# Conditioning projections: one-column products moved from inside two feed-forward parts to the waits of two layer norms

## The reference, cut to what matters

```
x = layer_norm(ALPHA * x + 0.5 * swiglu(x, w_gu, w_down), g, b)    # four times
shared = nsa_shared_kv(x, nsa_w_kv, ...)                           # after layer 0
```

```
def ada_params(cond, w, b):
    m = jax.nn.silu(cond) @ w + b      # w: 1024 x 3072
    return jnp.split(m, 3, axis=-1)    # shift, scale, gate
hl = rmsnorm(xl, norm_g[l]) * (1.0 + scale) + shift
```

## Time and profile before

| | us |
|---|---|
| median of 3 runs | 2537.26 (2536.59 to 2537.66) |
| span of the profiled execution | 2533.9 |
| TensorE busy | 2492.8 (98%) |
| DVE busy | 1446.8 (57%) |
| POOL busy | 1081.5 (43%) |
| ACT busy | 955.0 (38%) |

### The profile page before, as it was taken

The page is one execution under the profiler, slowest core; times in us unless marked ns, Lnnn a source line. Parts: engine busy times, 40 slices in busy tenths (PEclk is TensorE's granted clock), DMA queues, the critical chain, the costliest instruction groups (busy, mean ns, idle before and its releaser), DMA issues.

```text
span 2533.9 us, 34230 instructions
## 1 busy us (share of the span) xinstructions
PE 2492.8 (98%) x12668; PEld 2007.6 (79%) x12668; DVE 1446.8 (57%) x2058; ACT 955.0 (38%) x1500; POOL 1081.5 (43%) x718
## 2 busy tenths in 40 slices
PE   8999999999999999999999999999999999999999
PEld 7888887657788888788888777788888888787887
DVE  6545556575755645555654648674343364896553
ACT  5222224464422223432222468653222244463322
POOL 3978874203749942323633402264020056032401
PEclk9999999999999999999999999999999999999999
DMA  8345445311444455344442221145333326533332
GB/s 212 95 128 150 126 123 138 97 34 51 125 125 132 149 145 133 107 133 125 141 150 85 82 80 34 51 147 168 107 107 94 94 75 191 190 124 112 92 92 67
DMA packets 439259, 292.07 MB, mean 115 GB/s; under 512 B 34371, under 2 KB 420218, under 8 KB 435802
## 3 DMA queue, kind: packets, MB, share of 16 engines
q1 hardware_dynamic: 422042, 212.38, 29.9%
q0 software_dynamic: 17088, 77.93, 9.8%
HBM read 272.50 MB, written 20.92 MB: 116 GB/s over the span
## 4 chain that ended last, share of the span: by engine, by line
PE 88%; POOL 5%; DVE 3%; ACT 2%; issue 1%; DMA 0%; SPq 0%; ACTq 0%; POOLq 0%; DVEq 0%
PE ps L770 40%; PE ps L775 20%; PE ps L853 5%; PE ps L880 4%; PE ps L1078 2%; PE ps L1066 2%; POOL SW L3145 1%; POOL NS L3143 1%; PE ps L1502 1%; POOL NS L3142 1%; DVE wl L2298 1%; PE ps L1093 1%; PE ps L1355 1%; PE ps L1259 1%; PE ps L1085 1%
## 5 line engine op out<-in xcount | busy, mean ns | idle before, releaser
L2298 DVE TENSOR_TENSOR wl<-raw,wh 128x1024 fp32r<-128x1024 f32 x376 | 617.9, 1644 | 839.8 <-ACT wh L1728 836.6
L1728 ACT ACTIVATE wh<-raw 128x1024 fp32r<-128x1024 f32 x385 | 408.2, 1060 | 1320.5 <-PE ps L775 1159.5
L770 PE MATMUL ps<-XH,wh 128*128 128x512 f32 x1832 | 719.2, 393 | 0.5 <-ACT wh L1728 0.5
L770 PE MATMUL ps<-XL,wh 128*128 128x512 f32 x1832 | 713.2, 389 | 0.0
L775 PE MATMUL ps<-XH,wl 128*128 128x512 f32 x1832 | 453.2, 389 | 0.0
L770 PEld LDWEIGHTS ps<-XH,wh 128*128 128x128 f32 x1832 | 344.0, 188 | 76.8 <-issue 4.9
L770 PEld LDWEIGHTS ps<-XL,wh 128*128 128x128 f32 x1832 | 344.0, 188 | 72.8 <-issue 2.2
L775 PEld LDWEIGHTS ps<-XH,wl 128*128 128x128 f32 x1832 | 343.9, 188 | 71.7 <-issue 0.4
L3264 POOL TENSOR_TENSOR NS<-AW,CS 128x2048 f32<-128x2048 f32 x32 | 116.8, 3649 | 215.8 <-PE ps L1173 207.1
L770 PE MATMUL ps<-HH,wh 128*128 128x512 f32 x528 | 207.2, 392 | 0.0
L770 PE MATMUL ps<-HL,wh 128*128 128x512 f32 x528 | 205.5, 389 | 0.0
(11 more groups left out here) (538 smaller groups left out, 3929.2 us busy)
## 6 DMA issues: line engine op xcount, KB each, us to landing
raw<-in_ffn_w_gu SPq DMA_DIRECT2D x176, 512.0 KB, 3.9
raw<-in_ffn_w_down SPq DMA_DIRECT2D x64, 512.0 KB, 3.9
AW<-in_ada_w POOLq DMA_DIRECT2D x24, 1024.0 KB, 7.3
raw<-in_ffn_w_down SPq DMA_DIRECT2D x32, 384.0 KB, 3.5
BS<-s_b POOLq DMA_DIRECT2D x12, 1024.0 KB, 5.4
raw<-in_odd_w_in SPq DMA_DIRECT2D x24, 512.0 KB, 3.8
raw<-in_even_w_in SPq DMA_DIRECT2D x22, 512.0 KB, 4.7
s_w<-SW POOLq DMA_DIRECT2D x12, 512.0 KB, 6.4
```

The source lines that it names most:

```text
L770: pe.matmul(ps[:, p % 4, 0:n], wh[:, p % 2, k * P:(k + 1) * P], x[:, k, 0:n], start=k == 0 and x is hi, stop=False)
L1728: act.activation(wh[:, p % 2, :], raw[:, p % 4, :], ACT.Copy).then_inc(w_hi, 1)
L2298: dve.tensor_tensor(wl[:, p % 2, :], raw[:, p % 4, :], wh[:, p % 2, :].bitcast(F32), ALU.subtract).then_inc(w_lo, 1)
```

## The change

TensorE no longer runs the conditioning products inside the feed-forward parts, but for the first eight of layer 0 (slabs 0 and 1), which stay at ffn1's first fill. The rest go into the norms of ffn1 and ffn2 and into the pair of panels after each. In norm: 2, 1, 4, 10 products (ffn1) or 2, 1, 4, 9 (ffn2). The last three of these numbers take the place of the warming products 2, 3, 6. In the pair: 5, 5, 5 after the first three chunks of kv, or 3, 3, 2 after those of nsa.

As the operands wait longer, each has a slot of its own: AS0 (layer 0, a new tile beside AW, in space used later by KS, KW, VS, VW, KCB, VCB and others), and the first 12 rows of the tile W1 (layer 1). POOL no longer waits for `ada_used` inside `load_ada`. It clears KCB and VCB later, after a wait for `ada_used`. ACT waits for all 12 sums before the last projection's first cast, since the squares it writes share space with POOL's products. `ada_used` now counts once per layer.

```diff
+                    AS0 = pb("AS0", [P, 16, 2 * P])
...
+                    AS1 = W1[1][:, 0:12, :]
...
+        ADA_ORDER = [[(n, c, e) for n in range(12) for c in range(2) for e in range(ada_conditions(layer, n))] for layer in range(2)]
+        ADA_EARLY = (8, 0)
+        ADA_SPARE = {"ffn1": (0, (2, 1, 4, 10, 5, 5, 5)), "ffn2": (1, (2, 1, 4, 9, 3, 3, 2))}
...
                         mm = product(1, k - behind, wh, lo)
+                    beside(k)
...
                 token_means(4, ACQ, True, False)
+                ada_spare(stage, 0)
                 pe.wait_ge(*taken_at(stage, last))
                 token_means(5, XT[:, KD - 1, :], False, True).then_inc(ln_mean, 1)
-                warm(free, 2)
+                if not ada_spare(stage, 1):
+                    warm(free, 2)
...
-                warm(free, 3)
+                if not ada_spare(stage, 2):
+                    warm(free, 3)
...
-                if beside is nothing:
+                if not ada_spare(stage, 3) and beside is nothing:
                     warm(free, 6)
...
+            def ada_products(layer, first, last):
+
+                for n, c, e in ADA_ORDER[layer][first:last]:
+                    m = 2 * n + c
+                    mm = pe.matmul(ps[:, 6, 2 * m + e:2 * m + e + 1], ada_slot(layer, n, e)[:, c * P:(c + 1) * P], ONES[:, 0:1], start=True, stop=True)
+                if last == len(ADA_ORDER[layer]):
                     mm.then_inc(ada_used, 1)
 
+            def ada_fill(f):
+
+                if f == 0:
+                    pe.wait_ge(ada_part, 2)
+                    ada_products(0, 0, ADA_EARLY[0])
+
+            def ada_spare(stage, piece):
+
+                if stage not in ADA_SPARE:
+                    return False
+                layer, counts = ADA_SPARE[stage]
+                if piece == 0:
+                    pe.wait_ge(ada_part, 12 * layer + 12)
+                first = ADA_EARLY[layer] + sum(counts[:piece])
+                ada_products(layer, first, first + counts[piece])
+                return True
+
             def ffn2_fill(f):
-                ada_fill(1, f)
...
-            ffn("ffn1", lambda f: ada_fill(0, f))
+            ffn("ffn1", ada_fill)
...
-            panels("kv", 6, split_at("kv"))
+            panels("kv", 6, split_at("kv"), beside=lambda k: ada_spare("ffn1", 4 + k) if k < 3 else None)
...
-            panels("nsa", 9, split_at("nsa"), after=gates_t)
+            panels("nsa", 9, split_at("nsa"), after=gates_t, beside=lambda k: ada_spare("ffn2", 4 + k) if k < 3 else None)
...
+                if j == 0 and stage in ADA_SPARE:
+                    act.wait_ge(ada_part, 12 * ADA_SPARE[stage][0] + 12)
...
-                dve.wait_ge(ada_used, 12 * (layer + 1))
+                dve.wait_ge(ada_used, layer + 1)
...
-                    wait(pool, ada_used, 12 * layer + n - 1)
...
-                        ins = pool.tensor_tensor(AS[:, n % 2, e], prod[:, 0], prod[:, 1], ALU.add)
+                        ins = pool.tensor_tensor(ada_slot(layer, n, e), prod[:, 0], prod[:, 1], ALU.add)
...
             norm("ffn1")
+            pool.wait_ge(ada_used, 1)
+            pool.memset(KCB[:], 0.0)
+            pool.memset(VCB[:], 0.0).then_inc(zeros, 1)
```

More of the change, by code:

```diff
@@ L603, in ada_conditions, with ada_slot @@
             return 2 if layer == 0 and n < 8 else 1
+        def ada_slot(layer, n, e):
+            if layer == 1:
+                return AS1[:, n, :]
+            if n < 2:
+                return AS[:, n, e]
+            return AS0[:, 2 * n - 4 + e if n < 8 else n + 4, :]
+        ADA_ORDER = [[(n, c, e) for n in range(12) for c in range(2) for e in range(ada_conditions(layer, n))] for layer in range(2)]
+        ADA_EARLY = (8, 0)
+        ADA_SPARE = {"ffn1": (0, (2, 1, 4, 10, 5, 5, 5)), "ffn2": (1, (2, 1, 4, 9, 3, 3, 2))}
         def nothing(k):
@@ L838, in early_pair, with pair @@
                     beside(k)
-            def pair(stage, hi, lo, need, nk=8, n=T, off=0, behind=3, order=range(KD)):
+            def pair(stage, hi, lo, need, nk=8, n=T, off=0, behind=3, order=range(KD), beside=nothing):
                 p = BASE[stage] + off
@@ L900, in down_pair, with panels @@
                 mm.then_inc(pe_panel, 1)
-            def panels(stage, count, need, hi=XH, lo=XL, nk=8, after=None, within=None, order=range(KD)):
+            def panels(stage, count, need, hi=XH, lo=XL, nk=8, after=None, within=None, order=range(KD), beside=nothing):
                 if need is not None:
-                    pair(stage, hi, lo, need, nk, order=order)
+                    pair(stage, hi, lo, need, nk, order=order, beside=beside)
                 for j in range(2, count):
@@ L1162, in s5_fill @@
                 mm.then_inc(s5_z, 1)
[L1164 to L1173, removed]
-                    mm.then_inc(ada_used, 1)
+            def ada_products(layer, first, last):
[3 more added lines that the diff above has]
+                if last == len(ADA_ORDER[layer]):
+                    mm.then_inc(ada_used, 1)
+            def ada_fill(f):
[11 more added lines that the diff above has]
+                return True
             def ffn2_fill(f):
-                ada_fill(1, f)
                 if f == 0:
@@ L3276, in _ @@
             pool.memset(ZB[:, :, :, :, NCMP:], 0.0).then_inc(zeros, 1)
[L3277 to L3280, removed]
+            pool.memset(H1[:], 0.0).then_inc(zeros, 1)
             pool.wait_ge(cs_ready, 1)
```

## The result

| | before | after |
|---|---|---|
| median, us | 2536.3 (2533.3 to 2537.7, 10 runs) | 2542.0 (2540.3 to 2543.8, 10 runs) |
| span of the profiled execution, us | 2533.9 | 2540.7 |

The changed kernel takes 1.0023 of the time before (95% interval 1.0015 to 1.0032): 5.7 us slower, where 7 us faster was forecast. The time is outside the range. In the changed kernel the lines have moved: products 770 and 775 are now 784 and 789, 853 is 867, 880 is 895, 990 and 996 are 1005 and 1011, 1173 is 1186; ACT's cast 1728 is 1758, DVE's `wl` 2298 is 2330 and HL 2318 is 2350, POOL's multiplication 3264 is 3295.

What follows compares the result with a forecast made beforehand. TensorE, busy 98% of the span, was taken to bound the kernel. 12.4 - 0.3 + 0.2 - 0.7 = 11.6 us off, less 4.6 for the clock, gave 7.0 off the median 2537.26: 2530.2 us, range 2523.0 to 2533.0.

Steps and rivals of the forecast that it cites:

- removed from the parts: Products leaving the feed-forward parts: 7.2 us off in ffn1 and 5.2 in ffn2, 12.4 in sum, firm within 0.3.
- kv pair at full clock: Fifteen products added after kv's first three chunks make the pair end 0.3 us late (from -0.2 to 1.2).
- sum at full clock: All terms with TensorE at 2.4 GHz throughout: 11.6 us off, giving 2525.7 us.
- POOL in DVE's and the queues' way: At the projections, unbroken POOL work slows DVE, so TensorE waits for the last hidden chunk: 0.7 us for all such places.
- clock in both pairs: TensorE's clock falls to half for 6.8 us, costing 3.2 us in kv and 1.4 in nsa, together 4.6.
- ACT's new wait, POOL's memsets: ACT's wait before the last projection never waits; POOL's wait behind the norm holds only memsets wanted some 20 us later.
- the bound of about 4 "at one place": Upper bound on a projection's stall: wl and HL each behind a whole POOL operation of 3.61 us.
- rival 3: POOL's unbroken run makes DVE late at three projections, 2.5 us each above 0.7, at full clock: 2532.5 us; chance 0.08.
- the first rival: The clock holds in both pairs because the products close the gaps: 2525.7 us; chance 0.32.
- no idle left in kv: In the kv pair TensorE has no idle left, so 6.8 us at half speed costs 3.2 us.
- Rival 4: Clock stays at half beyond the two pairs; with 17 us in each, 16 us lost, 2541.7 us; chance 0.04.
- the signs that I had listed: Wrong if TensorE idles in projections with DVE as releaser; right if kv's last product comes 19 to 24 us after norm's first mean.

Runs made afterwards that it cites:

- e3: The changed kernel with conditioning products 128 columns wide and POOL again waiting for TensorE's progress at the old panels; 2524.9 us.
- e2: The changed kernel with POOL again waiting for TensorE's progress at the panels where it waited before; 2533.3 us.
- e1: The changed kernel with each conditioning product 128 columns wide instead of one; 2533.4 us.
- e5: e1 with POOL's loads of cmp_w held back until TensorE has finished panel 54 of ffn1; 2530.7 us.
- e12: The kernel before, without the warming products in the norms of ffn1 and ffn2, nothing in their place; 2536.7 us.
- e10: e5 with POOL's multiplication of 2048 columns cut into four of 512 and its first addition into two of 512; 2523.0 us.
- e4: The kernel before with the new slots alone: POOL no longer waits, products stay in the feed-forward parts, warming products in the norms; 2540.4 us.
- e8: e2 with conditioning products 128 columns wide in the pairs and one column inside the norms; 2526.8 us.
- e11: e1 with POOL's slabs released two panels later than in e2 and POOL's operations cut short as in e10; 2522.3 us.

## Why the prediction was wrong

Its terms, and what the runs showed:

| term | predicted | shown |
|---|---|---|
| removed from the parts | 12.4 off | 13.0 off, and 1.1 where a stall of before also went |
| kv pair at full clock | 0.3 late | 0.8 late (e3) |
| sum at full clock | 11.6 off | 11.3 off (e3), after 0.8 lost near 880 |
| POOL in DVE's and the queues' way | 0.7 of that sum | 8.7 (changed kernel less e2) |
| clock in both pairs | 4.6 | 8.6 (changed kernel less e1; 8.5 in their traces) |
| ACT's new wait, POOL's memsets | nothing | nothing |

That the sum at full clock came out within 0.3 is partly luck: the 1.1 of the stall that went stood in no term, and it covers what the pair lost more.

**The step that failed is the one on POOL and DVE.** It had the mechanism, and the bound of about 4 "at one place"; its value of 0.7 was sized at one instance, the down projection near 871, where the changed kernel then lost only 0.2. Three things were wrong with that. It took the place where POOL had been by chance of its waits as the place where it would be. The first down projection of ffn2 got no sum of its own: 3.4 idle and 1.6 of clock behind it, plus 2.0 in the projection ahead of it, and that was the largest part. And POOL's queue was not followed to its end: behind the 20 multiplications stand the loads of `cmp_w`, and freeing POOL moves these 60 us forward, into the weights of ffn1 (2.7, e5).

**The argument against rival 3 was empty.** It said that POOL was already busy 125.5 of 135 us with TensorE busy for all of them. But that stretch is ffn1, and there POOL does no harm to HL in either kernel (1.5 us in both between 795 and 880). The harm is in ffn2, where POOL stood idle for 60 us before. In all, the amount of POOL's work does not change; its phase does. The 207.1 us of waits, which I read as time given away, kept POOL's long operations out of the way of HL. e2 gives the waits back, at no cost, and the 8.7 are gone. Rival 3 came nearest in mechanism, with 7 us against 8.7, though DVE was late at one projection and not at three, and the loads did the rest. My chance of 0.08 was far too small, and it was priced together with a clock that holds. Its sum was also off: 3 x 2.5 is 7.5, which gives 2533.2.

**The clock term had the right mechanism and the wrong size.** The first rival, that it holds, is refuted (0.54 and 0.50 where the kernel before had 1.00). The fall was sized by the only one of before, 6.8 us, which ended when TensorE got dense. Here thirty one-column records stand between the split chunks, so TensorE stays thin for longer: 13.65 us in the changed kernel and 17 in e2. I had also let the products keep their 0.1 us per record at half clock; ten took 1.99. The "no idle left in kv" of the prediction was right, and e12 shows its other side. Rival 4, the clock at half beyond both pairs, was worked out with 17 us in each; the kv pair came to 13.65 to 17 and nsa to 6.8, so it was half true, and without POOL's part it would have given a kernel that is still faster (e2, by 2.8 us). That its price of 2541.7 lies beside the measured 2542.0 is chance. Of the signs that I had listed, idle TensorE inside a projection with DVE as releaser came, in ffn2; and the last product of the kv pair came 28.3 us after the norm's first mean, not 19 to 24.

**The Trainium skill** on the page "TensorE: Matmul & The Clock Gate", table "Why this matters for your kernels", blames idle gaps. The stalls at 902 and 1162 of the changed kernel agree, each with a fall behind it (3.4 us at half); the stall of 2.0 in e1 near 899 had none. The fall in kv does not agree: TensorE was busy in all of 1018 to 1036.

The exclusive lock of the Trainium skill's page "SBUF — State Buffer", section "SBUF: two separate sides", agrees in part. HL ends 0.56 us behind POOL's multiplication of 3.62, as if it had run only then. But the page gives the lock to the operation that starts first, and by the records HL starts 0.53 us earlier and is held all the same; in e10 it is held through four operations of POOL.

**What stays open.** For POOL's part the traces of the changed kernel and of e2 differ by 9.1 us (2.8 in ffn1, 5.4 and 0.9 before and behind the start of ffn2's first down projection), where the medians say 8.7; runs of one kernel differ by more. Why POOL and DVE run in step, and why HL is held though it starts first, is not shown. In e4 a free POOL cost only 4.3, and the reason given there was not varied. Each statement on the clock rests on one profiled run per kernel. Why a fall of 3.4 us shows up in some executions in other places (442 in e2, 648 in e4, e5, e8 and e10) and not in others was not looked into, nor why the one near 2100 lasts 3.4 us in some and 10.3 in others.

## What to carry to other kernels

A wait that looks like lost time can be pacing. Before you take one away, list what the engine does next, operations and DMAs up to its next real wait, and ask at which phase of the other engines each will now fall. If filler is to keep the clock, make it wide: here a product of 128 columns cost the same step as one of a single column, and only the wide ones kept it in every profiled run. And a clock fall is to be priced by the slack around it: nothing where TensorE waits anyway, all of it where the waits have just been filled.

## What the runs showed of the hardware

- An fp32 product of 128 columns took the same step as one of one column: the product behind 20 records started 2.16 us after the first of them against 2.15 (e1, after). With 128 columns the clock stayed at 2.4 GHz in norm and pair of kv in all five profiled runs (e1, e3, e5, e10, e11); with 32 once it stayed and once it was at half for 10 us; with one it was at half for 14 to 17 us, TensorE being busy throughout.
- At half clock one-column products double as well: ten records step by 1.99 instead of 1.0.
- DVE's subtraction HL of 128x512 took 4.71 on average over eight when POOL multiplied 2048 columns at a stretch, and 0.69 where POOL had no such operation (six of the eight of before). With POOL's operations of 512 columns the median was 1.64, but two of eight stood behind a whole group of four (5.12 and 3.43).
- Beside over 4 MB of loads from POOL's queue, SP's loads of 512 KB took 22.2 us in the median instead of 3.9 (after, 870 to 920), and 14.4 in the kernel before.
